# Attention stage: low parts of the weight blocks and the large value difference move from VectorE to GpSimd, and ScalarE scales the blocks in place first

## The chip, the cores and the metric

The kernel runs on one core of a Trainium2 chip. The metric is the device time of one execution in microseconds (us), lower is better. The engines are TensorE (PE in profiles; PEld is its weight load), VectorE (DVE), ScalarE (ACT), GpSimd (POOL) and SyncE (SP, which issues most DMAs here). Each works through its own queue in order and waits on semaphores that others raise.

## The reference, cut to what matters

The model is one hybrid layer (a Mamba-2 mixer beside a stick-breaking attention, then a feed-forward part) followed by a second hybrid layer, over 1024 tokens and 16 meta tokens. Only the attention stage is touched:

```python
proj = xn @ w_in[l]
q, k, v = (proj[..., a:b].reshape(Bsz, L, SB_HEADS, SB_HEAD_DIM) for ...)   # 16 heads of 64
...
zlog = jnp.einsum('bqhd,bkhd->bhqk', qi, kp) * scale
log_beta = jax.nn.log_sigmoid(zlog)
log_keep = jnp.where(valid, log_beta - zlog, 0.0)
after = lax.cumsum(log_keep, axis=3, reverse=True) - log_keep
w = jnp.where(valid, jnp.exp(log_beta + after), 0.0)
o = jnp.einsum('bhqk,bkhd->bqhd', w, vp)
```

The kernel computes the same sum in another form. With keep = sigmoid(-z), the running product of keep along the keys is what is "left" of the stick; the output is a first value plus the products of what is left with the differences of neighbouring values. So it needs a scan (a running product) for each head and query block, and the differences v[t+1] - v[t] of the values, called `steps`.

## The kernel before, in words

All large matrix products are made from f16 halves: an f32 operand x is cut into a high part (x rounded to f16) and a low part (x minus the high part, as f16), and three products (high x high, high x low, low x high) are summed in PSUM. Weight blocks of 128x1024 f32 arrive by DMA in two slots `L.raw` (`wraw_z` in the profile), are multiplied by 64 (`WSCALE`), and cut into `L.hi` (`whi_z`) and `L.lo` (`wlo_z`).

`attention_phase` (L1072) interleaves two kinds of work; the work is woven. Eight pairs of heads are treated one after the other, with nine steps each (72 steps `s`), one for each block of 128 queries (and one for the 16 meta queries). The order of query blocks within a pair is written out in `ORDER` (L1026): the first step of a pair is the small meta block, the sixth is the widest with 1040 keys. Beside each step runs one group of the linear products that make q, k and v of later pairs: three groups use up one weight block, so every third step (the first, fourth and seventh of a pair) a new block is cut, four blocks ahead of the step's number divided by three, which is three steps before its first use. This is so for 23 blocks, b = 4 to 26; blocks 2 and 3 are cut by GpSimd alone at the start.

Each engine's order is written out by hand:

- TensorE (L1300 to L1310): `scores(s)` (z = q.k, L1255), half of a linear group (L1239 to L1241), then the other half, then `values(s - 2)` (L1286, L1289). `values` needs the two transposes of the "left" tiles, and the PSUM bank of step s - 4, which ScalarE's `store` (L1391) has emptied.
- ScalarE (L1418 to L1440): for both heads `odds` (L1345: sigmoid of the scores out of PSUM), `store(s - 3)`, `left_high` of the first head (L1359), `weight_high` in every third step (L1376), `place` (L1331: a linear group out of PSUM), now and then `chunk_high` (L1396), in a pair's first step `values_high` (L1370), `left_high` of the second head (L1359, L1362), in the fifth step of a pair `square` (L1384).
- VectorE (L1524 to L1542): two scans (L1505), `left_low` of the first head (L1464), in a pair's first step `v_steps` (L1513 to L1516), `low` (L1449, reads PSUM), `values_low` (L1471), `left_low` of the second head (L1461, L1464), `norm_chunk` (L1475) in a few steps, `weight_low` in every third (L1454), `add_square` (L1522) in some.
- SP (L1160 to L1167): the transposes of the "left" tiles (and of the values), each a DMA that waits for its low part, and in every third step the load of a weight block, which waits until the block two before it, which holds the same slot, has its low part (`L.cut`).
- GpSimd (L1203 to L1222): the first two blocks, eight low parts of normed chunks (`low`, L1187), for each pair the split of a small tile of meta values (`split_values`, L1197 to L1201), and at the end the first two blocks of the next linear layer (L1217 to L1222).

The high part on ScalarE scales as it rounds, and leaves `L.raw` as it was; the low part on VectorE scales `L.raw` again and subtracts:

```python
nc.scalar.activation(L.hi[:, w, :], L.raw[:, w, :], ACT.Copy, scale=WSCALE).then_inc(s_bhi, 1)
nc.vector.scalar_tensor_tensor(L.lo[:, w, :], L.raw[:, w, :], WSCALE, L.hi[:, w, :], ALU.mult, ALU.subtract).then_inc(L.cut, 1)
```

Of the kernel before, what the change touches and what calls it, by code (L numbers as in the profile page):

```python
# [10 lines left out]
ALU = mybir.AluOpType  # L11
ACT = mybir.ActivationFunctionType
# [5 lines left out]
SEQ, META = 1024, 16  # L18
T = META + SEQ
BANK = 512  # L20
NT = 3
# [6 lines left out]
PAIRS = HEADS // 2  # L28
# [5 lines left out]
WSCALE = 64.0  # L34
SLOTS = 2
# [979 lines left out]
QKV_B = 3 * PAIRS  # L1015
EARLY = 3
NSTEP = 9
STEPS = PAIRS * NSTEP
LAG = 2
MSTACK = 6 * META  # L1020
BY_POOL = 4
PASSES = (0, 0), (0, 1), (1, 0)
GROUPS = 3 * NT
# [3 lines left out]
V_SENT = [2 * NSTEP * p for p in range(PAIRS)]  # L1027
# [24 lines left out]
ATT = [Step(n) for n in range(STEPS)]  # L1052
# [3 lines left out]
NORMED_AT = {2: 3, 4: 4, 6: 5, 11: 6, 13: 7}  # L1056
# [15 lines left out]
def attention_phase(nc, S, L, Lo, N, qs, ks, v, zacc):  # L1072
# [5 lines left out]
    with Phase(nc) as ctx:  # L1078
        sem = lambda n: ctx.semaphore(f"att_{n}")
# [9 lines left out]
        steps, first_v = sb("v_steps", [P, T + META]), sb("v_first", [P, 2, NSTEP])  # L1089
# [3 lines left out]
        s_left_hi, s_left_lo = sem("left_hi"), sem("left_lo")  # L1093
        s_turned = [sem(f"left_turned{i}") for i in range(SENT_SIGNALS)]
        s_bhi, s_low, s_vhi, s_vlo = (sem(n) for n in ("block_hi", "low", "v_meta_hi", "v_meta_lo"))
        split = lambda x: (x.bitcast(F16)[:, 0:T], x.bitcast(F16)[:, T:2 * T])
        q16, k16 = [split(x) for x in qs], [split(x) for x in ks]
        zsq = N.rs[:, 0:FW]
# [25 lines left out]
        def landed(e):  # L1124
            return s_turned[e % SENT_SIGNALS], 16 * (e // SENT_SIGNALS + 1)
# [5 lines left out]
        with nc.Block() as block:  # L1131
# [37 lines left out]
            @block.gpsimd  # L1169
            def _(pool):  # L1170
                def cut(b, part):
                    w = b % SLOTS
                    raw, hi, lo = L.raw[:, w, :], L.hi[:, w, :], L.lo[:, w, :]
                    if part == 0:
                        pool.wait_ge(L.landed[w], 16 * (b // SLOTS + 1))
                        nc.gpsimd.tensor_scalar(raw, raw, WSCALE, 1.0, ALU.mult, ALU.mult).then_inc(L.step, 1)
                    elif part == 1:
                        pool.wait_ge(L.step, 2 * b + 1)
                        pool.wait_ge(s_lin, NT * (b - SLOTS + 1))
                        nc.gpsimd.tensor_scalar(hi, raw, 1.0, 1.0, ALU.mult, ALU.mult).then_inc(L.step, 1)  # L1180
                    else:
                        pool.wait_ge(L.step, 2 * b + 2)
                        nc.gpsimd.tensor_tensor(lo, raw, hi, ALU.subtract).then_inc(L.cut, 1)

                def low(k):
                    pool.wait_ge(N.used, k + 1)
                    nc.gpsimd.tensor_tensor(N.lo[:, k, 0:N.width], N.src[:, k, 0:N.width], N.hi[:, k, 0:N.width], ALU.subtract).then_inc(N.cut, 1)  # L1187

                thirds = [slice(2 * META * i, 2 * META * (i + 1)) for i in range(3)]

                def split_values(p):
                    high, again, low_ = (vm16[at, p % 2, :] for at in thirds)
                    pool.wait_ge(s_copied, p + 1)
                    pool.wait_ge(N.cut, NORMED_EARLY + sum(s < NSTEP * p for s in NORMED_AT))
                    if p >= 2:
                        pool.wait_ge(s_pv, NSTEP * (p - 1))
                    nc.gpsimd.tensor_copy(high, vm[:, :]).then_inc(s_vhi, 1)  # L1197
                    pool.wait_ge(s_vhi, 2 * p + 1)
                    nc.gpsimd.tensor_copy(again, vm[:, :]).then_inc(s_vhi, 1)
                    pool.wait_ge(s_vhi, 2 * p + 2)  # L1200
                    nc.gpsimd.tensor_tensor(low_, vm[:, :], high, ALU.subtract).then_inc(s_vlo, 1)  # L1201

                for b in (2, 3):  # L1203
                    for part in range(3):
                        cut(b, part)
                for k in range(NORMED_EARLY):
                    low(k)
                for p in range(PAIRS):
                    split_values(p)
                    pool.wait_ge(s_vlo, p + 1)  # L1210
                    for s, k in NORMED_AT.items():
                        if NSTEP * p <= s < NSTEP * (p + 1):
                            low(k)
                for s in range(SLOTS):
                    raw, hi, lo = (x[:, 1 - s, :] for x in (Lo.raw, Lo.hi, Lo.lo))
                    pool.wait_ge(Lo.landed[s], 16)
                    nc.gpsimd.tensor_scalar(raw, raw, WSCALE, 1.0, ALU.mult, ALU.mult).then_inc(Lo.step, 1)  # L1217
                    pool.wait_ge(Lo.step, 2 * s + 1)
                    pool.wait_ge(s_lin, NT * (QKV_B + EARLY - SLOTS + s + 1))
                    nc.gpsimd.tensor_scalar(hi, raw, 1.0, 1.0, ALU.mult, ALU.mult).then_inc(Lo.step, 1)  # L1220
                    pool.wait_ge(Lo.step, 2 * s + 2)
                    nc.gpsimd.tensor_tensor(lo, raw, hi, ALU.subtract).then_inc(Lo.cut, 1)  # L1222
# [90 lines left out]
            def _(act):  # L1313
# [50 lines left out]

                def values_high(p):
                    e = V_SENT[p]
                    act.wait_ge(s_steps, p + 1)
                    if p:
                        act.wait_ge(*landed(e - SENT_SLOTS))
                    nc.scalar.activation(left_part(e, 0, SEQ), steps[:, 0:SEQ], ACT.Copy).then_inc(s_left_hi, 1)  # L1370

                def weight_high(b):
                    w = b % SLOTS
                    act.wait_ge(L.landed[w], 16 * (b // SLOTS + 1))
                    act.wait_ge(s_lin, NT * (b - SLOTS + 1))
                    nc.scalar.activation(L.hi[:, w, :], L.raw[:, w, :], ACT.Copy, scale=WSCALE).then_inc(s_bhi, 1)  # L1376

                def square(p):
                    act.wait_ge(s_o, NSTEP * (p + 1))
# [63 lines left out]
            def _(dve):  # L1443
                def low(g):
                    p, kind, n = g // GROUPS, g // NT % 3, g % NT
                    w = min(TB, T - n * TB)
                    hi, lo = [backward(x, n) if kind else x[:, n * TB:n * TB + w] for x in (k16 if kind else q16)[p % 2]]
                    dve.wait_ge(s_out, g + 1)
                    nc.vector.scalar_tensor_tensor(lo, lin_ps(g)[:, 0:w], 1.0 / WSCALE, hi, ALU.mult, ALU.subtract).then_inc(s_low, 1)  # L1449

                def weight_low(b):
                    w = b % SLOTS
                    dve.wait_ge(s_bhi, b - BY_POOL + 1)
                    nc.vector.scalar_tensor_tensor(L.lo[:, w, :], L.raw[:, w, :], WSCALE, L.hi[:, w, :], ALU.mult, ALU.subtract).then_inc(L.cut, 1)  # L1454

                def left_low(n, a):
                    t, e = ATT[n], ATT[n].sent(a)
                    dve.wait_ge(s_left_hi, e + 1)
# [48 lines left out]
                def v_steps(p):  # L1507
                    dve.wait_ge(s_out, GROUPS * (p + 1))
                    if p:
                        dve.wait_ge(s_turn, p)  # L1510
                    if p >= 2:
                        dve.wait_ge(s_o, NSTEP * (p - 1))
                    nc.vector.tensor_tensor(steps[:, 0:SEQ], v[:, 1:SEQ + 1], v[:, 0:SEQ], ALU.subtract)  # L1513
                    nc.vector.tensor_tensor(steps[half(0), SEQ:T], v[half(0), SEQ + 1:T + 1], v[half(0), SEQ:T], ALU.subtract)
                    nc.vector.tensor_tensor(steps[half(1), T + META - 1:T - 1:-1], v[half(1), SEQ + 1:T + 1], v[half(1), SEQ:T], ALU.subtract)
                    nc.vector.tensor_copy(first_v[:, p % 2, :], v[:, 0:SEQ + 1:P]).then_inc(s_steps, 1)  # L1516
# [7 lines left out]
                for s in range(STEPS):  # L1524
                    scan(s, 0)
                    scan(s, 1)
                    if ATT[s].j:
                        left_low(s, 0)
                    if ATT[s].i == 0:
                        v_steps(ATT[s].p)  # L1530
                    if s + GROUPS in SPLIT:
                        low(s + GROUPS)
                    if ATT[s].i == 0:
                        values_low(ATT[s].p)
                    left_low(s, 1)
                    if s in NORMED_AT:
                        norm_chunk(NORMED_AT[s])
                    if s % NT == 0 and s // NT + BY_POOL < QKV_B + EARLY:
                        weight_low(s // NT + BY_POOL)
                    p = ATT[s].p - 1  # L1540
                    if p >= 1 and ATT[s].i == 6:
                        add_square(p)  # L1542
# [2586 lines left out]
```

## Time and profile before

| what | value |
|---|---|
| median of 3 runs | 2272.23 us (2267.42 to 2272.71) |
| profiled execution, its own time | 2265.52 us |
| its span | 2263.8 us |
| TensorE busy | 2155.3 us, 95% |
| VectorE busy | 1593.5 us, 70% |
| ScalarE busy | 992.3 us, 44% |
| GpSimd busy | 666.7 us, 29% |
| mean granted TensorE clock | 0.986 |

The attention steps lie between about 366 and 784 us of the span. Busy time of an engine counts its compute instructions from start to end, and an instruction that is held up inside the engine counts as busy for as long as that lasts. In a row of windows the columns after the length are the busy times of PE, PEld, DVE, ACT and POOL with instruction counts, then the granted clock of TensorE as a share of full speed, the DMA share and GB/s. In a row of a timeline the first number is the start, the second the time that the row covers (for "x2" two instructions in a row), and the bracket at the end is the idle time before it with what ended it.

### The profile page before, as it was taken

What the parts mean: (1) busy time and instruction counts of PE and PEld (TensorE: products, weight loads), DVE (VectorE), ACT (ScalarE), POOL (GpSimd) and SP (SyncE); (2) the same over time, 40 slices, a digit from 0 to 9 for tenths busy, and PEclk for the clock granted to TensorE, in tenths of its full rate; (3) what the DMA queues carried; (4) which work ended last, traced back from release to release, by engine and by line L of the source; (5) the groups of instructions that cost most, each with busy time, mean ns of one, the idle gap of its engine ahead of it and who ended that gap; (6) DMA issues with size and microseconds to landing.
All of it is one profiled execution on the core that took longest, in us unless ns stands there. A gap on an engine that the chain in (4) does not pass through costs nothing. (4 is left out here: it accounts for less than half of the span.)

```text
span 2263.8 us, 45652 instructions
## 1 busy us (share of the span) xinstructions
PE 2155.3 (95%) x19036; PEld 1440.5 (64%) x19036; DVE 1593.5 (70%) x2072; ACT 992.3 (44%) x1766; POOL 666.7 (29%) x417
## 2 busy tenths in 40 slices
PE   7999999999999899898999999999999999989998
PEld 4666665556666566566888885448744445568856
DVE  7876887988888655897888884246788676236654
ACT  3226765666666543524444443235544332124321
POOL 3555764211111220174333331000164533101160
PEclk9999999999999999999999999999999999999999
DMA  3113223668777622211112214326425432033422
GB/s 134 47 55 92 87 68 73 130 137 147 143 145 141 144 99 72 99 42 52 57 57 57 59 55 167 102 77 195 146 69 155 143 118 75 29 98 99 167 62 75
DMA packets 291189, 224.64 MB, mean 99 GB/s; under 512 B 204512, under 2 KB 254880, under 8 KB 289584
## 3 DMA queue, kind: packets, MB, share of 16 engines
q1 hardware_dynamic: 290992, 221.83, 36.2%
q8 instruction: 146, 2.39, 0.4%
q14 instruction: 51, 0.42, 0.1%
HBM read 148.86 MB, written 28.86 MB: 79 GB/s over the span
## 5 line engine op out<-in xcount | busy, mean ns | idle before, releaser
L1505 DVE TENSOR_TENSOR_SCAN att_left<-att_left,att_unseen_prefix 16x16 f32<-16x16 f32 (+5 forms) x144 | 179.2, 1284 | 15.7 <-ACT att_left L1345 15.7
L2918 PE MATMUL ps<-second_x_hi,whi_z 128*128 128x512 f16 (+1 forms) x480 | 179.0, 373 | 3.4 <-POOL wlo_z L2883 1.9
L1239 PE MATMUL ps<-x_hi,whi_z 128*128 128x348 f16 x560 | 175.8, 314 | 3.4 <-DVE att_q L1449 3.4
L2920 PE MATMUL ps<-second_x_hi,wlo_z 128*128 128x512 f16 (+1 forms) x480 | 178.7, 372 | 0.0
L2919 PE MATMUL ps<-second_x_lo,whi_z 128*128 128x512 f16 (+1 forms) x480 | 178.7, 372 | 0.0
L1241 PE MATMUL ps<-x_hi,wlo_z 128*128 128x348 f16 x560 | 174.6, 312 | 0.0
L1240 PE MATMUL ps<-x_lo,whi_z 128*128 128x348 f16 x560 | 174.5, 312 | 0.0
L1359 ACT ACTIVATE att_left_split<-att_left 128x256 f16<-128x256 f32 (+7 forms) x128 | 87.3, 682 | 141.0 <-DVE att_left L1505 122.3
L2883 POOL TENSOR_TENSOR wlo_z<-wraw_z,whi_z 128x1024 f16<-128x1024 f32 x28 | 65.7, 2348 | 179.9 <-ACT whi_z L3111 179.9
L1197 POOL CAST att_v_meta_split<-att_v_meta 32x128 f16<-32x128 f32 x8 | 37.9, 4740 | 255.5 <-ACT att_v_meta L1351 255.5
L1464 DVE SCALAR_TENSOR_TENSOR att_left_split<-att_left,att_left_split 128x256 f16<-128x256 f32 (+7 forms) x128 | 95.9, 749 | 0.2
L2208 PE MATMUL ps<-x_hi,whi_z 128*128 128x257 f16 (+1 forms) x288 | 80.4, 279 | 8.0 <-DVE gate_conv L2413 4.3
L3111 ACT ACTIVATE whi_z<-wraw_z 128x1024 f16<-128x1024 f32 x28 | 29.6, 1056 | 132.4 <-PE ps L2920 117.3
L219 PE MATMUL ps<-x_hi,whi_xbc 128*128 128x348 f16 x264 | 83.2, 315 | 4.6 <-DVE x_lo L487 4.6
L2918 PEld LDWEIGHTS ps<-second_x_hi,whi_z 128*128 128x128 f16 x480 | 46.9, 98 | 62.4 <-issue 6.3
L220 PE MATMUL ps<-x_lo,whi_xbc 128*128 128x348 f16 x264 | 83.0, 314 | 0.0
L221 PE MATMUL ps<-x_hi,wlo_xbc 128*128 128x348 f16 x264 | 82.9, 314 | 0.0
L1239 PEld LDWEIGHTS ps<-x_hi,whi_z 128*128 128x128 f16 x560 | 54.5, 97 | 42.2 <-issue 14.7
L2919 PEld LDWEIGHTS ps<-second_x_lo,whi_z 128*128 128x128 f16 x480 | 46.9, 98 | 53.5 <-issue 3.6
L2920 PEld LDWEIGHTS ps<-second_x_hi,wlo_z 128*128 128x128 f16 x480 | 46.9, 98 | 53.3
L1345 ACT ACTIVATE att_left<-ps 16x16 f32<-16x16 f32 (+5 forms) x144 | 79.0, 594 | 3.4 <-PE ps L1255 3.4
L2209 PE MATMUL ps<-x_lo,whi_z 128*128 128x257 f16 (+1 forms) x288 | 80.4, 279 | 0.0
(676 smaller groups left out, 6690.2 us busy)
## 6 DMA issues: line engine op xcount, KB each, us to landing
wraw_z<-in_w_second SPq DMA_DIRECT2D x30, 512.0 KB, 3.8
wraw_z<-in_w_up SPq DMA_DIRECT2D x26, 512.0 KB, 3.7
wraw_z<-in_w_qkv SPq DMA_DIRECT2D x24, 512.0 KB, 4.5
wraw_z<-in_w_down SPq DMA_DIRECT2D x20, 512.0 KB, 3.7
raw_down<-in_w_down SPq DMA_DIRECT2D x20, 512.0 KB, 4.0
seg<-dt_a_sums SPq DMA_DIRECT2D x18, 512.0 KB, 5.1
wraw_z<-in_w_up SPq DMA_DIRECT2D x36, 256.0 KB, 2.6
second_work<-parked_units SPq DMA_DIRECT2D x7, 1280.0 KB, 6.2
```

The lines of the kernel that those rows point to most:

```text
L219: nc.tensor.matmul(out, hi, xhi, start=(k == 0), stop=False)
L220: nc.tensor.matmul(out, hi, xlo, start=False, stop=False)
L221: return nc.tensor.matmul(out, lo, xhi, start=False, stop=(k == L.parts * L.kb - 1))
L1239: nc.tensor.matmul(lin_ps(g), hi, xhi, start=(kb == 0), stop=False)
L1240: nc.tensor.matmul(lin_ps(g), hi, xlo, start=False, stop=False)
L1241: last = nc.tensor.matmul(lin_ps(g), lo, xhi, start=False, stop=(kb == DB - 1))
L1359: last = nc.scalar.activation(left_part(e, 0, P * t.j), of_head(t, a, 0, P * t.j), ACT.Copy, scale=PSCALE)
L1464: last = nc.vector.scalar_tensor_tensor(low_, of_head(t, a, 0, P * t.j), PSCALE, high, ALU.mult, ALU.subtract)
L1505: nc.vector.tensor_tensor_scan(x, x, unseen, 1.0, ALU.mult, ALU.max).then_inc(s_scan, 1)
L2918: nc.tensor.matmul(out, hi, xhi, start=(j == 0), stop=False)
L2919: nc.tensor.matmul(out, hi, xlo, start=False, stop=False)
L2920: return nc.tensor.matmul(out, lo, xhi, start=False, stop=(j == DB - 1))
```

## The change

GpSimd gets a `weight_low` and a `v_apart`, and its loop runs over the steps. `weight_low` is a plain subtraction of two tiles now, since `L.raw` has been scaled by ScalarE in place: `weight_high` is two activations, the first from `L.raw` to `L.raw` with the factor 64, the second, after a wait for the first (`s_bscale`), from `L.raw` to `L.hi`. VectorE's `weight_low` is gone. `v_apart` makes the 128x1024 part of the value differences; it waits until the pair's last linear group has been placed, and until `values_low` of the pair before has read the old ones. ScalarE's `values_high` waits for it (`s_apart`). VectorE keeps the three small operations of `v_steps` (L1514 to L1516).

```diff
@@ GpSimd
-                for p in range(PAIRS):
-                    split_values(p)
-                    pool.wait_ge(s_vlo, p + 1)
-                    for s, k in NORMED_AT.items():
-                        if NSTEP * p <= s < NSTEP * (p + 1):
-                            low(k)
+                def weight_low(b):
+                    w = b % SLOTS
+                    pool.wait_ge(s_bhi, b - BY_POOL + 1)
+                    nc.gpsimd.tensor_tensor(L.lo[:, w, :], L.raw[:, w, :], L.hi[:, w, :], ALU.subtract).then_inc(L.cut, 1)
+
+                def v_apart(p):
+                    pool.wait_ge(s_out, GROUPS * (p + 1))
+                    if p >= 1:
+                        pool.wait_ge(s_left_lo, V_SENT[p - 1] + 1)
+                    nc.gpsimd.tensor_tensor(steps[:, 0:SEQ], v[:, 1:SEQ + 1], v[:, 0:SEQ], ALU.subtract).then_inc(s_apart, 1)
+
+                for s in range(STEPS):
+                    p = ATT[s].p
+                    if ATT[s].i == 0:
+                        v_apart(p)
+                    if s % NT == 0 and s // NT + BY_POOL < QKV_B + EARLY:
+                        weight_low(s // NT + BY_POOL)
+                    if ATT[s].i == 0:
+                        split_values(p)
+                        pool.wait_ge(s_vlo, p + 1)
+                    if s in NORMED_AT:
+                        low(NORMED_AT[s])
@@ ScalarE, values_high
-                    act.wait_ge(s_steps, p + 1)
+                    act.wait_ge(s_apart, p + 1)
@@ ScalarE, weight_high
                     act.wait_ge(L.landed[w], 16 * (b // SLOTS + 1))
+                    nc.scalar.activation(L.raw[:, w, :], L.raw[:, w, :], ACT.Copy, scale=WSCALE).then_inc(s_bscale, 1)
+                    act.wait_ge(s_bscale, b - BY_POOL + 1)
                     act.wait_ge(s_lin, NT * (b - SLOTS + 1))
-                    nc.scalar.activation(L.hi[:, w, :], L.raw[:, w, :], ACT.Copy, scale=WSCALE).then_inc(s_bhi, 1)
+                    nc.scalar.activation(L.hi[:, w, :], L.raw[:, w, :], ACT.Copy).then_inc(s_bhi, 1)
@@ VectorE
-                def weight_low(b):
-                    w = b % SLOTS
-                    dve.wait_ge(s_bhi, b - BY_POOL + 1)
-                    nc.vector.scalar_tensor_tensor(L.lo[:, w, :], L.raw[:, w, :], WSCALE, L.hi[:, w, :], ALU.mult, ALU.subtract).then_inc(L.cut, 1)
@@ VectorE, v_steps
-                    nc.vector.tensor_tensor(steps[:, 0:SEQ], v[:, 1:SEQ + 1], v[:, 0:SEQ], ALU.subtract)
@@ VectorE, the loop over steps
-                    if s % NT == 0 and s // NT + BY_POOL < QKV_B + EARLY:
-                        weight_low(s // NT + BY_POOL)
```

## Rows read from the trace of the kernel before

**Rows 1.** The page: its first line, and part 1, busy time by engine.

```profile
span 2263.8 us, 45652 instructions
...
PE 2155.3 (95%) x19036; PEld 1440.5 (64%) x19036; DVE 1593.5 (70%) x2072; ACT 992.3 (44%) x1766; POOL 666.7 (29%) x417
```

**Rows 2.** Windows: start:end, length, busy by engine (instructions), PEclk, DMA share, GB/s.

```profile
366.00:784.00 418.00, 392.61 (x4238) 247.63 (x4236) 359.72 (x460) 256.79 (x564) 77.33 (x36) 0.99 0.71 136
475.00:725.00 250.00, 243.09 (x2663) 154.06 (x2661) 217.52 (x292) 159.56 (x354) 30.40 (x15) 1.00 0.74 143
```

**Rows 3.** Costliest groups, attention only: line, engine, shapes, count, busy, mean ns, idle before.

```profile
L1454 DVE SCALAR_TENSOR_TENSOR wlo_z<-wraw_z,whi_z 128x1024 f16<-128x1024 f32 x23 | 27.9, 1214 | 0.0
L1376 ACT ACTIVATE whi_z<-wraw_z 128x1024 f16<-128x1024 f32 x23 | 23.9, 1040 | 0.0
L1513 DVE TENSOR_TENSOR att_v_steps<-att_v 128x1024 f32<-128x1024 f32 x8 | 9.5, 1190 | 0.0
```

**Rows 4.** Timeline of POOL: start, length, line, shapes, idle before and its releaser.

```profile
353.28 2.13 POOL L1183 TENSOR_TENSOR wlo_z<-wraw_z,whi_z 128x1024 f16<-128x1024 f32 x1
...
402.34 2.88 POOL L1187 TENSOR_TENSOR y_ssd_lo<-z,y_ssd_hi 128x1044 f16<-128x1044 f32 x1 [9.89 <-ACT y_ssd_hi L1396]
415.98 2.17 POOL L1187 TENSOR_TENSOR y_ssd_lo<-z,y_ssd_hi 128x1044 f16<-128x1044 f32 x1 [10.76 <-ACT y_ssd_hi L1396]
...
757.53 4.01 POOL L1222 TENSOR_TENSOR wlo_z<-wraw_z,whi_z 128x1024 f16<-128x1024 f32 x1
```

**Rows 5.** Timeline of DVE beside them, and one undisturbed pair of scans.

```profile
403.12 0.51 DVE L1449 SCALAR_TENSOR_TENSOR att_k_odd<-ps,att_k_odd 128x344 f16<-128x344 f32 x1
...
416.59 1.60 DVE L1461 SCALAR_TENSOR_TENSOR att_left_split<-att_left,att_left_split 128x32 f16<-128x32 f32 x1 [0.94 <-ACT att_left_split L1362]
...
553.56 4.54 DVE L1505 TENSOR_TENSOR_SCAN att_left<-att_left,att_unseen_prefix 128x1040 f32<-128x1040 f32 x2 [1.58 <-ACT att_left L1345]
...
757.03 6.69 DVE L1505 TENSOR_TENSOR_SCAN att_left<-att_left,att_unseen_prefix 128x1040 f32<-128x1040 f32 x2 [1.18 <-ACT att_left L1345]
```

**Rows 6.** Timeline of ACT, one fourth and one seventh step.

```profile
545.47 1.04 ACT L1376 ACTIVATE whi_z<-wraw_z 128x1024 f16<-128x1024 f32 x1
...
562.25 1.04 ACT L1376 ACTIVATE whi_z<-wraw_z 128x1024 f16<-128x1024 f32 x1
...
565.32 0.37 ACT L1391 ACTIVATE z<-ps,att_v_first 128x128 f32<-128x128 f32 x1
```

**Rows 7.** Timeline of DVE, the same two steps.

```profile
547.77 0.19 DVE L1461 SCALAR_TENSOR_TENSOR att_left_split<-att_left,att_left_split 128x32 f16<-128x32 f32 x1
...
564.46 0.19 DVE L1461 SCALAR_TENSOR_TENSOR att_left_split<-att_left,att_left_split 128x32 f16<-128x32 f32 x1 [1.34 <-ACT att_left_split L1362]
...
565.04 1.22 DVE L1454 SCALAR_TENSOR_TENSOR wlo_z<-wraw_z,whi_z 128x1024 f16<-128x1024 f32 x1
```

**Rows 8.** Timeline of PE where the seventh steps of three pairs end.

```profile
411.61 0.64 PE L1286 MATMUL ps<-att_left_turned,att_v_tokens 128*64 128x128 f16 x8 [2.89 <-ACT z L1391]
...
466.65 0.55 PE L1286 MATMUL ps<-att_left_turned,att_v_tokens 128*64 128x128 f16 x13 [2.34 <-ACT z L1391]
...
566.37 0.83 PE L1286 MATMUL ps<-att_left_turned,att_v_tokens 128*64 128x128 f16 x23 [1.43 <-ACT z L1391]
```

**Rows 9.** Timeline of ACT before a new pair.

```profile
522.43 0.44 ACT L1331 ACTIVATE att_v<-ps 128x344 f32<-128x344 f32 x1
```

**Rows 10.** Timeline of DVE before and in the first step of that pair.

```profile
523.08 0.80 DVE L1464 SCALAR_TENSOR_TENSOR att_left_split<-att_left,att_left_split 128x640 f16<-128x640 f32 x1
...
527.92 1.23 DVE L1471 TENSOR_TENSOR att_left_split<-att_v_steps,att_left_split 128x1024 f16<-128x1024 f32 x1 [0.47 <-ACT att_left_split L1370]
```

**Rows 11.** Windows around the first two stalls of rows 8.

```profile
410.00:414.00 4.00, 2.39 (x46) 2.42 (x48) 4.00 (x5) 1.01 (x4) 0.00 (x0) 0.62 0.76 138
464.00:468.00 4.00, 1.66 (x51) 1.38 (x48) 2.89 (x5) 2.57 (x7) 0.00 (x0) 1.00 0.98 187
```

**Rows 12.** Timeline of POOL, first step of splitting a pair's meta values.

```profile
531.51 4.25 POOL L1197 CAST att_v_meta_split<-att_v_meta 32x128 f16<-32x128 f32 x1 [43.17 <-ACT att_v_meta L1351]
```

More of the change, by code:

```diff
@@ L1095, in attention_phase @@
         s_bhi, s_low, s_vhi, s_vlo = (sem(n) for n in ("block_hi", "low", "v_meta_hi", "v_meta_lo"))
+        s_bscale, s_apart = sem("block_scaled"), sem("v_apart")
         split = lambda x: (x.bitcast(F16)[:, 0:T], x.bitcast(F16)[:, T:2 * T])
```

## The prediction, made before the change was run

> **What bounds the kernel now.** I read the page first. TensorE is busy for 95% of the span, VectorE for 70%, so TensorE is the first candidate [rows 1]. The change touches attention alone, so I cut that stage out by windows: it lasts 418.0 us, with TensorE busy for 392.6, VectorE for 359.7, ScalarE for 256.8 and GpSimd for 77.3 [rows 2]. TensorE is idle for 25.4 us in all. In the middle, 475 to 725 us, it is idle for only 6.9 of 250 us, so there TensorE sets the pace and VectorE, 87% busy, is close behind it [rows 2]. That makes the first bound plain: however much VectorE is relieved, this stage can give back little more than TensorE's idle time.
>
> Then I looked at where TensorE does stall. The timeline shows the same place in pair after pair: a value product waits for ScalarE's `store` (L1391) at the end of the seventh step of a pair, for 2.89, 2.34 and 1.43 us in the three pairs shown [rows 8] (six of the seven pairs that have weight work in this step stall there). The row of ScalarE ahead of the third of them shows why: `weight_high` at 562.25, the rest of the step behind it, then the store at 565.32, and TensorE goes on at 566.37 [rows 6, 8]. So in the seventh step ScalarE's queue is on the path.
>
> **ScalarE: one more pass for each block.** 23 blocks get a second activation of 128x1024. The present one takes 1.04 us [rows 3]. The new one differs only in writing f32 in place; the trace has no row of it in this place, and I take the same 1.04, between 0.95 (back to back they overlap a little, but the second now waits for the first, which takes that away) and 1.2. That is 24 us on an engine with 161 us free [rows 2], so it costs nothing as work. It costs as latency: behind `weight_high` in ScalarE's queue stand `place`, the second `left_high`, and the next step's `odds` and `store`. VectorE waits for that `left_high`: in the seventh step it had stood idle 1.34 us for it already [rows 7], so each microsecond there is one more for VectorE, and one more for TensorE behind the store.
>
> **VectorE: what is taken away.** 23 low parts of 1.21 us and 8 differences of 1.19 us, 37.4 us by busy time [rows 3]; neighbours overlap by about 0.08, so 1.13 us each from start to start, 35 us of its queue.
>
> **GpSimd: what is added, and what it takes from VectorE.** The same 31 operations as TENSOR_TENSOR on GpSimd. Alone, this form takes 2.13 us [rows 4]. 31 x 2.13 = 66 us, and GpSimd was idle for 341 us of the stage, so as work that is free too. But the two engines do not run such work side by side. In rows 4 and 5: GpSimd holds 415.98 to 418.15, and a 128x32 operation of VectorE, which takes 0.19 us elsewhere [rows 7], starts at 416.59 and ends at 418.19, when GpSimd does. At 757.53 GpSimd takes 4.01 us instead of 2.13, having waited for the scan that ran, and VectorE's two scans take 6.69 us instead of 4.54, 2.15 more: GpSimd got in between them and VectorE waited for the whole of it. An operation of VectorE that reads PSUM does run beside it: 0.51 us at 403.12 within GpSimd's 402.34 to 405.22. So each moved operation costs VectorE up to 2.13 us, less the time that VectorE is idle or works from PSUM, in exchange for 1.13.
>
> The Trainium skill ("SBUF — State Buffer", section "Who interferes with whom") has this as a rule: a VectorE instruction with two SBUF inputs contends with a GpSimd instruction that reads SBUF, and whichever starts second blocks fully. By that rule the move costs more than it frees; without it the 35 us would be plain relief. The trace agrees with the rule: 2.15 us more for the scans.
>
> Now by step, each with its rows:
> - Seventh step (7 of them). The high part now ends near 562.25 + 0.95 + 1.04 = 564.3, so GpSimd holds 564.3 to 566.4. VectorE wants L1461 at 564.46 + 1.04 = 565.5 and gets it at 566.4: 1.98 later; less 1.13 for the low part gone from 565.04: 0.85 late [rows 6, 7].
> - Fourth step (8). High part done at 545.47 + 1.99 = 547.5, GpSimd to 549.6. VectorE's L1461 moves from 547.77 to 549.6, 1.83; less 1.13: 0.7 late [rows 6, 7].
> - First step (8). The value difference can go as soon as the last `place` ends, 522.43 + 0.44 = 522.9 [rows 9], while VectorE scans. It gets in at 523.1 and holds off VectorE's 0.80 us operation to 525.2 [rows 10]; the low part of the block does the same once more. 2 x 2.13 - 2 x 1.13 = 2.0, of which I take 1.0 as covered: the idle 0.47 us at 527.92 [rows 10] and, by estimate, as much again in shorter gaps of the step. 1.0 late. `values_low` moves back too, and the transpose of the values behind it in SP's queue; I count that within the 1.0.
>
> So VectorE's chain gets later by 1.0 + 0.7 + 0.85 = 2.55 us in a full pair, though it has less work. Not all of this reaches TensorE. The seventh step's 1.04 on ScalarE does, at once, since TensorE waits there. Of the 1.7 carried from the first and fourth steps I count half, 0.85, as TensorE, the pace maker between stalls, takes the rest out of its lead. 7 x (1.04 + 0.85) = 13.2. The last pair has no seventh-step block and TensorE's cover is thin at its end, so its 1.7 counts in full: 14.9 us.
>
> **Waits and queues.** `weight_high` waits for its own scale pass; that is in the 1.04. SP's load of the next block waits for the low part; it used to be issued after VectorE's work, and now after GpSimd's, at about the same time, with the next transpose in SP's queue due only after two scans: nothing, at most 1 us in the first pair, where GpSimd's norm chunks stand ahead of the low part. The block is used three steps later, so TensorE doesn't wait for it. GpSimd's meta values (`split_values`) come behind a low part in its queue; they have three steps.
>
> **The clock.** After the 2.89 us stall the granted clock was 0.62 in 410 to 414; with the 2.34 us stall it stayed at 1.00 in 464 to 468 [rows 8, 11]. The fall costs 0.38 x 4 = 1.5 us. Stalls that are 1.9 us longer, 3.3 to 4.2 us, would pass 2.89 in several pairs. While TensorE is slow the others catch up, so most of this comes out of the next stall; I count one fall, 1.5 us, with bounds 0 and 7 x 1.5 = 10.5.
>
> **Sum.** 14.9 + 1.5 = 16.4 us on the profiled execution's 2265.5 us (its span is 2263.8 [rows 1]), so 2281.9. The median of the runs, 2272.2, lies 6.7 above the profiled one; on it, 2288.6, and I say 2288.5, slower by 0.7%. For this mechanism alone: from 7 x 1.04 = 7 to 19.6 (all of 7 x 2.55 + 1.7) + 10.5 = 30 us, so 2279 to 2302.
>
> **Rivals.**
> 1. Relief wins (faster). GpSimd may be kept out by a VectorE that works back to back: its first CAST of a pair's meta values took 4.25 us [rows 12], where VectorE's scans stood at their full length. If the new operations only slip into gaps, VectorE loses little, and the 1.13 gained cancels ScalarE's 1.04 in fourth and seventh steps, while the first step keeps 1.13 + 1.13 - 1.04 = 1.2. That gives back 8 x 1.2 = 10 us at the most, 2262; it can't be much more, since TensorE is idle for 25 us in all, some of it at the end. Against it: the only such TENSOR_TENSOR that met two scans won after one [rows 4, 5]. Chance 0.16.
> 2. TensorE covers it (no change). VectorE is later by 2.5 us a pair, but TensorE's 97% in the middle hides it and only ScalarE's share in some stalls shows: 0 to 6 us, 2275. For it: the pace maker is TensorE. Against it: the stalls of rows 8 say that the loop is caught up with once in each pair. Chance 0.2.
> 3. It does more harm: the lateness all shows and the clock falls in each pair, 20 to 30 us, 2297. This is the upper end of my own mechanism. Chance 0.17.
>
> My forecast itself has 0.47. A change of under 0.3% (6.8 us) can't be told from none here. Faster 0.16; within, 0.2; slower, 0.47 + 0.17 = 0.64. The range is 2263 to 2304: it leaves out the best of rival 1 and the worst of rival 3.
>
> **What would show it.** In the profile after: GpSimd's two forms 31 times, with means of 2.2 to 3 us; VectorE's L1461 and scans longer on average though its total may fall by less than 37 us; longer idle time of VectorE before L1461; TensorE's stall at the end of the seventh step grown by 1 to 2 us; a granted clock below 1.00 in more places. Wrong if VectorE's busy time falls by the full 37 us and the scans keep their length: then GpSimd found gaps, and rival 1 holds. Wrong as well if the seventh-step stall stays as it is.

## The result, and the profile after

The changed kernel takes 2286.69 us (median of 6 runs, 2284.22 to 2287.89) against 2270.70 us before (6 runs, 2267.02 to 2272.71): ratio 1.0075, 95% interval 1.0065 to 1.0086. It is slower by 16.0 us; 16.4 were forecast. The profiled execution, 2286.97 us, is near its median, where the one of before was 5 us below its own, so the traces differ by more (21.3 us of span) than the runs do.

The page after, first line and part 1:

```profile
span 2285.1 us, 45679 instructions
...
PE 2155.9 (94%) x19036; PEld 1440.6 (63%) x19036; DVE 1599.2 (70%) x2041; ACT 1015.2 (44%) x1789; POOL 717.4 (31%) x448
```

TensorE's work is the same, VectorE's share did not fall though 31 operations left it, and GpSimd has 50.7 us more (its new operations are 65.0 us; the cast of the meta values, which was held up for long before, fell from 37.9 to 23.4). Next the attention stage cut by windows, the first two pairs of heads, the next five together, and the last one with the end (columns as in rows 2). Before:

```profile
366.00:423.00 57.00, 51.07 (x490) 31.70 (x489) 51.39 (x60) 32.99 (x76) 16.55 (x7) 0.94 0.61 114
423.00:476.00 53.00, 48.11 (x529) 30.34 (x527) 47.84 (x63) 33.95 (x74) 11.05 (x5) 1.00 0.69 135
476.00:725.00 249.00, 242.09 (x2656) 153.39 (x2655) 216.52 (x288) 158.56 (x351) 30.40 (x15) 1.00 0.75 144
725.00:784.00 59.00, 51.34 (x570) 32.21 (x568) 43.97 (x52) 31.30 (x67) 19.33 (x9) 0.96 0.68 125
```

After, with the whole stage as the last row:

```profile
366.00:430.00 64.00, 53.16 (x540) 32.64 (x538) 54.94 (x56) 38.77 (x80) 25.86 (x12) 1.00 0.54 101
430.00:487.00 57.00, 47.34 (x518) 29.92 (x516) 49.36 (x59) 35.73 (x75) 18.88 (x9) 1.00 0.64 126
487.00:746.00 259.00, 243.40 (x2664) 154.16 (x2660) 217.42 (x269) 173.63 (x367) 64.82 (x35) 1.00 0.73 138
746.00:805.00 59.00, 48.74 (x537) 30.48 (x534) 42.73 (x49) 32.70 (x69) 19.77 (x11) 0.97 0.67 125
366.00:805.00 439.00, 392.64 (x4247) 247.20 (x4245) 364.45 (x429) 280.83 (x588) 129.32 (x67) 1.00 0.68 129
```

TensorE is busy for 392.6 us in both [rows 2]. Its idle time grew from 25.4 to 46.4 us: by 4.9 in the first pair (57.0 - 51.1 before, 64.0 - 53.2 after), 4.8 in the second, 8.7 in the next five together and 2.6 in the last. VectorE's busy time went up, from 359.7 to 364.5 us, though work of 37.4 us had been taken away. So 42 us of something else is inside its instructions. The groups of the stage say what. After, put in order by engine (line, engine, shapes, count, busy and mean ns, idle before):

```profile
L1212 POOL TENSOR_TENSOR wlo_z<-wraw_z,whi_z 128x1024 f16<-128x1024 f32 x23 | 49.8, 2163 | 165.2 <-ACT whi_z L1395 165.2
...
L1218 POOL TENSOR_TENSOR att_v_steps<-att_v 128x1024 f32<-128x1024 f32 x8 | 15.2, 1906 | 51.5 <-ACT att_v L1348 51.5
...
L1392 ACT ACTIVATE wraw_z<-wraw_z 128x1024 f32<-128x1024 f32 x23 | 23.9, 1040 | 0.0
...
L1519 DVE TENSOR_TENSOR_SCAN att_left<-att_left,att_unseen_prefix 16x16 f32<-16x16 f32 (+5 forms) x144 | 180.0, 1290 | 16.7 <-ACT att_left L1362 16.7
...
L1478 DVE SCALAR_TENSOR_TENSOR att_left_split<-att_left,att_left_split 128x256 f16<-128x256 f32 (+7 forms) x128 | 108.8, 850 | 0.2
L1475 DVE SCALAR_TENSOR_TENSOR att_left_split<-att_left,att_left_split 128x32 f16<-128x32 f32 (+1 forms) x72 | 32.6, 452 | 47.7 <-ACT att_left_split L1379 47.3
...
L1529 DVE COPY att_v_first<-att_v 128x9 f32<-128x9 f32 x8 | 10.8, 1347 | 0.1
```

Before, the VectorE groups that answer to the last four (L1519, L1478, L1475, L1529):

```profile
L1505 DVE TENSOR_TENSOR_SCAN att_left<-att_left,att_unseen_prefix 16x16 f32<-16x16 f32 (+5 forms) x144 | 179.2, 1284 | 15.7 <-ACT att_left L1345 15.7
...
L1464 DVE SCALAR_TENSOR_TENSOR att_left_split<-att_left,att_left_split 128x256 f16<-128x256 f32 (+7 forms) x128 | 95.9, 749 | 0.2
...
L1461 DVE SCALAR_TENSOR_TENSOR att_left_split<-att_left,att_left_split 128x32 f16<-128x32 f32 (+1 forms) x72 | 20.7, 287 | 35.5 <-ACT att_left_split L1362 34.8
...
L1516 DVE COPY att_v_first<-att_v 128x9 f32<-128x9 f32 x8 | 1.4, 174 | 0.1
```

The 32-column operation of `left_low` went from a mean of 287 to 452 ns, the wide one from 749 to 850, and a copy of nine columns from 174 to 1347 ns. They have the same work as before. The scans kept their length. VectorE's wait for ScalarE before the 32-column operation grew by 12.5 us (34.8 to 47.3). GpSimd's 31 operations have means of 1906 and 2163 ns, that is, GpSimd hardly ever waited: it was VectorE that did. The timelines show it. GpSimd in a seventh step, then VectorE beside it:

```profile
577.98 2.12 POOL L1212 TENSOR_TENSOR wlo_z<-wraw_z,whi_z 128x1024 f16<-128x1024 f32 x1 [15.22 <-ACT whi_z L1395]
```

```profile
578.84 1.31 DVE L1475 SCALAR_TENSOR_TENSOR att_left_split<-att_left,att_left_split 128x32 f16<-128x32 f32 x1 [2.20 <-ACT att_left_split L1379]
```

VectorE stands idle for 2.20 us where it was 1.34 [rows 7], then an operation of 0.19 us takes 1.31 and ends at 580.15, when GpSimd's ends (580.10). The longer idle time (0.86 us) and the hold (1.12 us) make 1.98 us, just what the prediction had for this step. ScalarE in the same step, with the new pass at 575.77, and TensorE where it stalls:

```profile
575.77 1.04 ACT L1392 ACTIVATE wraw_z<-wraw_z 128x1024 f32<-128x1024 f32 x1
576.84 1.06 ACT L1395 ACTIVATE whi_z<-wraw_z 128x1024 f16<-128x1024 f32 x1
```

```profile
579.88 0.83 PE L1303 MATMUL ps<-att_left_turned,att_v_tokens 128*64 128x128 f16 x23 [1.65 <-issue]
```

Around a new pair, GpSimd's value difference and low part, and VectorE beside them:

```profile
535.61 1.90 POOL L1218 TENSOR_TENSOR att_v_steps<-att_v 128x1024 f32<-128x1024 f32 x1 [8.23 <-ACT att_v L1348]
539.37 2.13 POOL L1212 TENSOR_TENSOR wlo_z<-wraw_z,whi_z 128x1024 f16<-128x1024 f32 x1 [1.85 <-ACT whi_z L1395]
```

```profile
535.75 2.45 DVE L1478 SCALAR_TENSOR_TENSOR att_left_split<-att_left,att_left_split 128x640 f16<-128x640 f32 x1
...
539.48 2.04 DVE L1529 COPY att_v_first<-att_v 128x9 f32<-128x9 f32 x1
```

The `left_low` of 0.80 us [rows 10] takes 2.45, and the copy of nine columns 2.04.

### The profile page after: what moved, and what is told of

It is laid out like the page before. It is cut to its first block and busy times, and to the rows that moved or that the text cites. A ratio compares the mean times of both kernels' runs of the same rounds, so it can differ in the third digit from the quotient of the medians.

```text
span 2285.1 us, 45679 instructions
## 1 busy us (share of the span) xinstructions
PE 2155.9 (94%) x19036; PEld 1440.6 (63%) x19036; DVE 1599.2 (70%) x2041; ACT 1015.2 (44%) x1789; POOL 717.4 (31%) x448
## 5 line engine op out<-in xcount | busy, mean ns | idle before, releaser
L1519 DVE TENSOR_TENSOR_SCAN att_left<-att_left,att_unseen_prefix 16x16 f32<-16x16 f32 (+5 forms) x144 | 180.0, 1290 | 16.7 <-ACT att_left L1362 16.7
L2894 POOL TENSOR_TENSOR wlo_z<-wraw_z,whi_z 128x1024 f16<-128x1024 f32 x28 | 65.7, 2348 | 181.0 <-ACT whi_z L3122 181.0
L1478 DVE SCALAR_TENSOR_TENSOR att_left_split<-att_left,att_left_split 128x256 f16<-128x256 f32 (+7 forms) x128 | 108.8, 850 | 0.2
L1212 POOL TENSOR_TENSOR wlo_z<-wraw_z,whi_z 128x1024 f16<-128x1024 f32 x23 | 49.8, 2163 | 165.2 <-ACT whi_z L1395 165.2
L1303 PE MATMUL ps<-att_left_turned,att_v_tokens 128*64 128x128 f16 x1728 | 60.4, 220 | 30.1 <-issue 12.6
L1303 PEld LDWEIGHTS ps<-att_left_turned,att_v_tokens 128*64 128x64 f16 x1728 | 50.9, 110 | 49.1 <-issue 36.5
```

Of the source, the lines that this page charges most:

```text
L1303: nc.tensor.matmul(o_ps(n)[half(a)], vt[:, t.p % 2, (NSTEP - 1) * (x + 1) - t.j + m, half(a)], turned[t.slot][:, keys_at(t, a) + y * t.j + ...
L1478: last = nc.vector.scalar_tensor_tensor(low_, of_head(t, a, 0, P * t.j), PSCALE, high, ALU.mult, ALU.subtract)
L1519: nc.vector.tensor_tensor_scan(x, x, unseen, 1.0, ALU.mult, ALU.max).then_inc(s_scan, 1)
```

## The experiments

Each was timed in five rounds beside the kernel before on the same chip. The differences in us of `e1` to `e4` are worked out from the ratio, the others from the medians; for one run the two ways agree to within 1.2 us (for `e1` 10.9 and 10.1, for `e3` 5.0 and 4.4, for `e4` 9.1 and 9.5).

**1. Taking the change apart.** `e1_scale_only` has only ScalarE's extra pass:

```diff
+ nc.scalar.activation(L.raw[:, w, :], L.raw[:, w, :], ACT.Copy, scale=WSCALE).then_inc(s_bscale, 1)
+ act.wait_ge(s_bscale, b - BY_POOL + 1)
- nc.vector.scalar_tensor_tensor(L.lo[..], L.raw[..], WSCALE, L.hi[..], ALU.mult, ALU.subtract)
+ nc.vector.tensor_tensor(L.lo[..], L.raw[..], L.hi[..], ALU.subtract)
```

> Only ScalarE's extra in-place pass (23 x 1.04 us) is added; the low part stays on VectorE as a plain subtraction of the same length, the value difference stays too. My theory (queue latency on ScalarE in every third step, plus the shared access of VectorE and GpSimd): the pass by itself costs 7 x 1.04 in the seventh steps and part of it in the fourth, so 7 to 12 us slower than before. Rival A (the cost is all in GpSimd's hold on VectorE): within 3 us of before. Rival B (the cost is all latency on ScalarE): the whole 16 us.

Measured: 2278.48 us, ratio 1.0048 (1.0033 to 1.0063), 10.9 us slower. The extra pass alone costs two thirds of the whole, on an engine that is 61% busy in the stage. VectorE waits for ScalarE before the 32-column operation for 43.8 us (34.8 before), and its operations keep their length:

```profile
L1464 DVE SCALAR_TENSOR_TENSOR att_left_split<-att_left,att_left_split 128x32 f16<-128x32 f32 (+1 forms) x72 | 20.7, 287 | 43.9 <-ACT att_left_split L1363 43.8
```

`e2_weights_only` is the change with the large value difference back on VectorE.

> The change without its value part: scale pass on ScalarE, low parts on GpSimd, the large value difference back on VectorE. My theory: 0.7 + 0.85 + about 0.5 per pair, so 11 to 14 us slower than before. If the value part carries most of the cost (it starts under the last scan of a pair and holds up the first step), it comes out at 4 to 8 us.

Measured: 2283.01 us, ratio 1.0065 (1.0050 to 1.0079), 14.7 us slower, just above what I expected. The weights carry nearly all of it.

`e3_values_only` is the kernel before with `v_apart` on GpSimd and nothing else.

> The large value difference alone goes to GpSimd; weight blocks as before. My theory: a hold of 2.13 us for 1.13 us of relief, half covered: 8 x 0.5 = 4 us slower, between 2 and 7. Rival (relief wins, as the first step has idle time): 2 to 5 us faster.

Measured: 2272.74 us, ratio 1.0022 (1.0013 to 1.0031), 5.0 us slower. Eight operations moved to an idle engine, and the time rises. Its trace has the hold too: the wide `left_low` group takes 107.5 us where it took 95.9, and the scans keep their 179.1.

`e4_weights_no_scale` takes the scale pass out of `e2`:

```diff
- nc.scalar.activation(L.raw[..], L.raw[..], ACT.Copy, scale=WSCALE).then_inc(s_bscale, 1)
+ lin_scale = lambda g: 1.0 / WSCALE if g < NT * BY_POOL else 1.0    # in place() and low()
```

> Low parts on GpSimd, but no scale pass: the woven blocks are cut without the factor 64, and their sums are read out with factor 1. The value difference stays on VectorE. It has GpSimd's hold without ScalarE's latency. My theory: the hold costs 1 us more than it frees, less the cover, so 3 to 8 us slower than before, and some 7 us faster than the variant with the scale pass. Rival B (all is ScalarE's latency): 3 to 8 us faster than before.

Measured: 2277.81 us, ratio 1.0040 (1.0025 to 1.0054), 9.1 us slower, a little over what I expected. So rival B falls: with no extra pass anywhere the move still loses. Its trace has the mark of the hold, a mean of 471 ns for the 32-column operation where `e1` had 287:

```profile
L1465 DVE SCALAR_TENSOR_TENSOR att_left_split<-att_left,att_left_split 128x32 f16<-128x32 f32 (+1 forms) x72 | 33.9, 471 | 42.7 <-ACT att_left_split L1371 41.7
```

The parts add to 10.9 + 9.1 + 5.0 = 25.0 us, and together they cost 16 to 17. Most of the difference is between the first two, which cost 14.7 together (`e2`) and not 20.0: a delay that ScalarE causes and one that GpSimd causes in the same step lie over each other in part, as in the seventh step above, where GpSimd's hold begins while VectorE still waits for ScalarE.

**2. Is the scale pass latency, or work?** `e11_scale_early` is `e1` with `weight_high` moved to where ScalarE waits for VectorE's scan:

```diff
-                    if s % NT == 0 ...: weight_high(s // NT + BY_POOL)     # behind left_high(s, 0)
+                    if s % NT == 0 ...: weight_high(s // NT + BY_POOL)     # ahead of left_high(s, 0)
```

> e1_scale_only with both passes of weight_high moved ahead of the first head's left_high, where ScalarE waits for VectorE's scan in any case. VectorE keeps all its work, GpSimd gets none. If e1's 10.9 us are latency in ScalarE's queue, they fall to 0 to 5 us here; and then it is GpSimd's hold, not the scale pass, that keeps e7 at 15 us. If the extra pass costs by itself (shared access, more work), they stay at 8 us or more.

Measured: 2268.69 us, ratio 1.0001 (0.9992 to 1.0010). The 10.9 us are gone with the same instructions in another order. ScalarE in the seventh step now goes from the two passes straight into `left_high`, before which it stood idle for 1.43 us in the kernel before:

```profile
558.85 1.06 ACT L1376 ACTIVATE wraw_z<-wraw_z 128x1024 f32<-128x1024 f32 x1
559.95 1.06 ACT L1379 ACTIVATE whi_z<-wraw_z 128x1024 f16<-128x1024 f32 x1
560.91 0.51 ACT L1360 ACTIVATE att_left_split<-att_left 128x384 f16<-128x384 f32 x1
```

`e6_high_earlier` does the same move in the kernel before, with its single pass.

> The kernel before, with ScalarE's weight_high moved ahead of the first head's left_high, where ScalarE stands idle for 1.43 us (seventh step) or 0.98 us (fourth step) waiting for VectorE's scan. All work stays. If latency on ScalarE's queue behind weight_high is what makes the seventh-step stalls, 3 to 8 us faster than before. If it is not, within 2 us.

Measured: 2265.44 us, ratio 0.9986 (0.9977 to 0.9995), 3.3 us faster: the one complete version here that beats both kernels. It also puts `e11` in its place: the move is worth 3.3 us without any extra pass, so in the early place the pass seems still to cost about 3.4 us (ratios 1.0001 and 0.9986, from two chips; the intervals overlap from 0.9992 to 0.9995, so this is not certain). Of the 10.9 us, then, some 7.5 were the place in the queue, and the move itself pays for the rest in `e11`.

`e7_after_high_earlier` does it in the changed kernel.

> The changed kernel with both passes of weight_high moved ahead of the first head's left_high. ScalarE's idle time there covers some 1.4 of 2.0 us. My theory: the latency part of the cost (the scale pass alone cost 10.9 us) goes for the most part, GpSimd's hold stays: 4 to 9 us slower than before, that is 7 to 12 us faster than the changed kernel. If GpSimd's hold then falls on the scans, where VectorE has no idle time at all, less is won: 10 to 14 us slower than before.

Measured: 2284.16 us, ratio 1.0067 (1.0053 to 1.0081), 15.4 us slower: no better than the changed kernel, and both of my ranges missed. The latency went and the hold took its place: VectorE's wait for ScalarE before the 32-column operation fell from 47.3 to 35.1 us, and its two `left_low` groups together grew from 141.4 (116.6 in the kernel before) to 150.4. GpSimd's operation now starts before VectorE's first `left_low` instead of in VectorE's idle time, GpSimd first and VectorE after it:

```profile
572.64 2.13 POOL L1212 TENSOR_TENSOR wlo_z<-wraw_z,whi_z 128x1024 f16<-128x1024 f32 x1 [17.29 <-ACT whi_z L1395]
```

```profile
573.01 2.18 DVE L1478 SCALAR_TENSOR_TENSOR att_left_split<-att_left,att_left_split 128x384 f16<-128x384 f32 x1 [0.21 <-ACT att_left_split L1376]
```

The `left_low` of 0.54 us takes 2.18, and SP's transpose comes after it.

**3. The relief and the hold by themselves.** `e10_relief_only` leaves out all but 8 of the 1024 columns of the 23 low parts.

> The kernel before, with the low parts of the 23 woven blocks left out but for 8 of their 1024 columns (VectorE is spared about 1.05 us each, nothing goes to GpSimd or ScalarE). It says what the relief of VectorE is worth by itself. If TensorE sets the pace in most of the stage, 24 us less on VectorE give back 4 to 9 us. If VectorE were the bound, 15 to 24 us. If its work there is hidden altogether, 0 to 3 us.

Measured: 2263.87 us, ratio 0.9977 (0.9968 to 0.9986), 4.8 us faster. 24 us less on VectorE give back a fifth. That is about the most that the weight part of the change could have won.

`e8_hold_wide` adds a hold and relieves nobody: GpSimd makes each low part once more.

```diff
+ pool.wait_ge(s_lowered, b - BY_POOL + 1)
+ nc.gpsimd.tensor_tensor(L.lo[..], L.raw[..], L.hi[..], ALU.subtract).then_inc(L.cut, 1)
```

> A hold without relief: VectorE makes the low parts as before (without the factor 64 in the woven blocks), and GpSimd then makes the same 128x1024 low part once more, 23 times, before the block counts as cut. Nothing else is added. If GpSimd's subtraction keeps VectorE out for its 2.13 us, VectorE's scans stand longer by about 2.1 us in 23 steps and the time rises by 20 to 45 us. If the engines run side by side, 0 to 3 us, since GpSimd is idle for 340 us of the stage and the block is used three steps later.

Measured: 2319.90 us, ratio 1.0225 (1.0211 to 1.0239), 51.2 us slower, above my range. It is no clean hold, though: TensorE waits 29.2 us at L1299 for the split of the meta values, which stands behind the new operation in GpSimd's queue, where the kernel before waits 3.3 us. So some 26 of the 51 us are that queue. `e9_hold_narrow` was to be its control.

> The control to e8_hold_wide: the same code and waits, but GpSimd's second subtraction covers 8 of the 1024 columns. The theory of the hold: what e8 lost (51 us) is gone, within 3 us of before. If the loss in e8 came from the later signal that the block is cut, or from the waits themselves, some 20 us or more stay.

Measured: 2281.02 us, ratio 1.0049 (1.0036 to 1.0063), 12.3 us slower: missed. The trace shows why. GpSimd's 8-column operation takes 4.89 us in a pair's first step, and the split of the meta values, for which TensorE waits at L1299, stands behind it; TensorE goes on when the split has ended (545.81). GpSimd, then TensorE:

```profile
537.55 4.89 POOL L1213 TENSOR_TENSOR wlo_z<-wraw_z,whi_z 128x8 f16<-128x8 f32 x1 [14.38 <-DVE wlo_z L1464]
...
545.33 0.48 POOL L1203 TENSOR_TENSOR att_v_meta_split<-att_v_meta,att_v_meta_split 32x128 f16<-32x128 f32 x1
```

```profile
545.91 0.17 PE L1299 MATMUL ps<-att_left_turned,att_v_meta_split 96*128 96x16 f16 x1 [1.62 <-issue]
```

Six such stalls of 1.16 to 3.35 us make 10.4 us. `e12_narrow_free` takes the queue away, with SP's load no longer gated by GpSimd and the split ahead of the small operation, and `e13_wide_free` is the same with 912 columns.

```diff
- sp.wait_ge(L.cut, b - SLOTS + 1)
+ sp.wait_ge(s_lowered, b - SLOTS - BY_POOL + 1)
- nc.gpsimd.tensor_tensor(lo, raw, hi, ALU.subtract).then_inc(L.cut, 1)
+ nc.gpsimd.tensor_tensor(lo, lo, prefix[:, P:P + n], ALU.add).then_inc(L.cut, 1)    # zeros; behind split_values
```

> e9 with both things that its small operation stood in front of taken away: SP's load of the next block no longer waits for it, and in a pair's first step GpSimd's split of the meta values comes ahead of it (it now adds a tile of zeros to 8 columns of the low part, so that it reads nothing that the load overwrites). In e9's trace TensorE waits 10.4 us in six first steps for the split (L1299), which stands behind an operation of 4.9 us on GpSimd. If that queue is what e9 lost, this is within 3 us of before; if the small operation costs by itself (its access, its signals), 8 to 12 us stay.

> The same with 912 columns instead of 8: a pure hold, 23 times some 1.9 us, with nothing queued behind it. If GpSimd keeps VectorE out, 25 to 42 us slower than before; if e8's 51 us were mostly queues behind GpSimd, 3 to 12 us.

Measured: `e12` 2267.70 us, ratio 0.9998 (0.9987 to 1.0008); `e13` 2288.98 us, ratio 1.0098 (1.0077 to 1.0120), 21.5 us slower, a little under my range. Only the width differs in the code. The scans and GpSimd's operation, in `e12`:

```profile
L1519 DVE TENSOR_TENSOR_SCAN att_left<-att_left,att_unseen_prefix 16x16 f32<-16x16 f32 (+5 forms) x144 | 178.4, 1279 | 15.7 <-ACT att_left L1359 15.7
...
L1217 POOL TENSOR_TENSOR wlo_z<-wlo_z,att_unseen_prefix 128x8 f16<-128x8 f16 x23 | 15.2, 663 | 169.4 <-DVE wlo_z L1468 168.8
```

and in `e13`:

```profile
L1519 DVE TENSOR_TENSOR_SCAN att_left<-att_left,att_unseen_prefix 16x16 f32<-16x16 f32 (+5 forms) x144 | 216.8, 1545 | 15.4 <-ACT att_left L1359 15.4
...
L1217 POOL TENSOR_TENSOR wlo_z<-wlo_z,att_unseen_prefix 128x912 f16<-128x912 f16 x23 | 55.9, 2432 | 157.2 <-DVE wlo_z L1468 156.5
```

VectorE's scans, with nothing changed about them, are 38.4 us longer, so GpSimd keeps VectorE out. The 21.5 us are not the price of that alone. With the split ahead of it, GpSimd's operation of a pair's first step ends just as TensorE wants the block, and TensorE waits for it eight times (L1253 is a linear product), which is not so in `e12`:

```profile
PE ps L1253 <- POOL wlo_z L1217: 8.9, 8, 1.8
```

TensorE is idle for about 19 us more than in `e12`, and 8.9 of them are this wait. No run here has the hold by itself, free of every queue.

## Why the prediction was right, point by point

- **What bounds the stage: right.** `e10` gives back 4.8 of 24 us, so TensorE sets the pace in most of it and VectorE is close behind.
- **GpSimd keeps VectorE out: right, and the main reason with the extra pass.** 31 operations of about 2.1 us are 65 us; 42 us of that appeared inside VectorE's instructions, against 37 us taken off. In the seventh step L1461 came 1.98 us later, as forecast, and at a new pair the 0.80 us operation was held for 1.65. Rival 1 fell. It had one thing right: GpSimd can be held off by a busy VectorE. But in the changed kernel its operations start when ScalarE signals. In fourth and seventh steps VectorE is then idle for the most part, waiting for ScalarE too; in first steps the value difference gets in where VectorE's scans end, and the low part most often between small operations. The scans, which I expected to be longer, kept their length (179.2 and 180.0 us): the hold fell on the operations behind them.
- **ScalarE's latency: right in kind, undersized.** I counted 7 x 1.04 = 7.3 us directly, and in the fourth step only what the pass does to GpSimd's start; alone it costs 10.9. `e6` and `e11` together show that about 7.5 of that is place in the queue.
- **The hold without the pass: undersized too.** My rows give next to nothing for it in two of three steps: without the 0.95 to 1.04 us that the pass adds, GpSimd's hold makes VectorE later by 0.9 to 1.0 us in fourth and seventh steps and the relief takes 1.13 off. That leaves 8 times 0.5 to 1 us in the first steps, 4 to 8 us at VectorE, of which my own rule passes on half (for `e4` I then expected 3 to 8). `e4` costs 9.1. The hold lies ahead of `left_low`, for which SP's transpose waits, and the relief behind it, at the end of VectorE's step; that this order is why 24 us of relief give only 4.8 (`e10`) was not tested.
- **Half of the carried lateness reaches the end: not shown.** `e13` loses 21.5 us to holds of 44 us in all, but 8.9 us of TensorE's waits there are for GpSimd's own operation. In `e10` a fifth of the relief came through.
- **The per-pair sum: near in the total of the runs, wrong in its spread.** The forecast for the stage was 14.9 us without the clock; the medians differ by 16.0 and the two traces by 21.0. TensorE's idle time grew by 4.9 and 4.8 us in the first two pairs, 1.7 on average in the next five and 2.6 in the last, where 1.9 and 1.7 had been forecast. The first two pairs have GpSimd's and ScalarE's norm chunks beside the rest. That these make the difference was not tested apart.
- **Where TensorE stalls: wrong.** The seventh-step stall was to grow by 1.9 us. It went from 1.43 [rows 8] to 1.65 in the pair shown, from 2.89 to 2.24 in the first, and over all pairs from 10.2 to 11.4 us. The prediction had named "stays as it is" as a sign of being wrong, and by that sign this part of it fails. The time is lost at other places: waits of `scores` for the scores' sigmoid grew from 4.4 to 12.2 us, and waits of `values` for transposes and without a named releaser from 8.9 to 24.6, while those put down to `store` fell from 8.4 to 3.1. Stalls at the end of fourth steps alone grew from 1.5 to 7.9 us. TensorE's waits before:

```profile
PE ps L1286 <- ACT z L1391: 8.4, 6, 2.9
PE ps L1286 <- DMA att_left_turned<-att_left_split: 5.4, 3, 3.0
...
PE ps L1255 <- ACT att_left L1345: 4.4, 5, 2.5
```

and after (L1303 is `values`, L1272 `scores`):

```profile
PE ps L1303 <- issue: 12.6, 12, 2.3
PE ps L1272 <- ACT att_left L1362: 12.2, 11, 3.0
PE ps L1303 <- DMA att_left_turned<-att_left_split: 12.0, 9, 3.0
PE ps L1303 <- ACT z L1410: 3.1, 2, 2.8
```

  One stall at the end of a fourth step, where TensorE waits for a transpose:

```profile
556.19 0.81 PE L1303 MATMUL ps<-att_left_turned,att_v_tokens 128*64 128x128 f16 x22 [1.89 <-DMA att_left_turned<-att_left_split]
```

  The loop of ScalarE, VectorE and the transposes was late enough to stop TensorE in first and fourth steps, and by the seventh TensorE was late as well, which would explain why the stall there kept its size; that link is argued from the traces and was not tested. My sum needed only that the lateness show once per pair, so it survived the wrong place.
- **The clock: wrong sign, small.** I added 1.5 us for one more fall. The granted clock was 0.94 in the first pair before and 1.00 after, though stalls there are longer in sum. The trace before has two falls there, behind stalls of 2.76 us (0.78 in 378 to 382) and 2.89 us; after, the longest stall in that pair is 2.75 us and the clock stays at 1.00. What decides was not tested. By estimate this gave back up to 57 x 0.06 = 3.4 us; a low clock costs nothing while TensorE stands idle.

With latency undersized by 3.6 us, the hold undersized as well, and the clock and the overlap of the two delays erring the other way, the total came within 0.4 us of the measured difference by luck. The mechanism (GpSimd keeps VectorE out, ScalarE's queue is late) is shown; the parts are good to 3 to 5 us each.

The rule of the Trainium skill that the prediction weighed ("SBUF — State Buffer", section "Who interferes with whom": two SBUF inputs on VectorE against a GpSimd instruction that reads SBUF) holds: `e13`'s scans are 38.4 us longer, and PSUM-reading operations beside a GpSimd one keep their 0.5 us. By the same section of the Trainium skill a one-input `copy` can contend too, in its two-port mode; the copy of nine columns that took 2.04 us at 539.48 agrees.

## What to carry to other kernels

Before work goes from VectorE to GpSimd, price it as 2.1 us taken from VectorE for each 1.1 us given back (128x1024, two inputs in SBUF), unless it falls into VectorE's idle or PSUM-reading time; an idle GpSimd doesn't make it free. An engine with 40% free time can still be on the path through its queue: ask what stands behind the added instruction, and try the place where the engine waits anyway, which here was worth 10.9 us with the extra pass and 3.3 without it. To price a hold by an added operation, look for whoever waits for that operation itself: `e8`, `e9` and `e13` all had such a wait in them. When a hold and a latency lie over each other, removing one only uncovers the other (`e7`), so test them apart.

## What the runs showed of the hardware that was not expected

A waiting GpSimd doesn't always get in between two VectorE instructions. At 757.53 it did, after one scan [rows 4, 5]. In `e8`, in a pair's first step, it waited through two scans and a third instruction, 4.7 us, until VectorE came to one that reads PSUM, and then held VectorE out for its 2.13 us; later in the pair the same instruction took 2.14 us with no wait. GpSimd in `e8`:

```profile
550.11 6.81 POOL L1213 TENSOR_TENSOR wlo_z<-wraw_z,whi_z 128x1024 f16<-128x1024 f32 x1 [14.28 <-DVE wlo_z L1464]
...
572.64 2.14 POOL L1213 TENSOR_TENSOR wlo_z<-wraw_z,whi_z 128x1024 f16<-128x1024 f32 x1 [13.59 <-DVE wlo_z L1464]
```

VectorE beside it (L1459 reads PSUM, L1471 is held to 556.97):

```profile
549.96 3.99 DVE L1515 TENSOR_TENSOR_SCAN att_left<-att_left,att_unseen_prefix 128x912 f32<-128x912 f32 x2
553.88 1.05 DVE L1474 SCALAR_TENSOR_TENSOR att_left_split<-att_left,att_left_split 128x896 f16<-128x896 f32 x1
554.86 0.50 DVE L1459 SCALAR_TENSOR_TENSOR att_q<-ps,att_q 128x348 f16<-128x348 f32 x1
555.29 1.68 DVE L1471 SCALAR_TENSOR_TENSOR att_left_split<-att_left,att_left_split 128x32 f16<-128x32 f32 x1
```

The 8-column operation of `e9` did the same (4.89 us for what takes 0.22 elsewhere). What decides between the two was not found; it needs a test with the gap between VectorE's instructions as the only variable. For a kernel it means that a small GpSimd operation, put at a busy time of VectorE, can block what stands behind it in GpSimd's own queue for 5 us.
